# A fused encoder layer on one core: shorter routing, tokens gathered in tiles of 128 slots, three of the four tiles gathered inside the first experts' blocks

## What is computed

```python
def hierarchical_moe(hn, w_rg, w_re, w1, w3, w2):
    p_group = softmax(xf @ w_rg);  g_idx = argmax(p_group);  g_gate = p_group[g_idx]
    fine = (xf @ w_re).reshape(n, MOE_GROUPS, MOE_PER_GROUP)[g_idx]
    top_v, top_i = lax.top_k(fine, MOE_TOPK)
    gate = g_gate * jax.nn.softmax(top_v, axis=-1)
    ...
    def expert_block(args):
        xblk, e = args
        return (jax.nn.silu(xblk @ w1[e]) * (xblk @ w3[e])) @ w2[e]
    ...
    y = zeros((n + 1, d_)).at[slot_tok].add(yb * slot_w[:, None])[:n]
```

## Time and profile before

| | us |
|---|---|
| median of 3 runs | 2014.64 (2013.08 to 2017.55) |
| the profiled execution, device time | 2014.21 |
| its span, first to last instruction | 2012.3 |
| PE busy | 1893.8 (94%) |
| DVE busy | 831.5 (41%) |
| ACT busy | 510.1 (25%) |
| weights and all else moved by DMA | 556.63 MB, mean 277 GB/s |

### The profile page before, as it was taken

How to read it: one execution, slowest core, us unless ns; L and a number is a source line. 1 busy time by engine, 2 the same in 40 slices (tenths; PEclk the granted TensorE clock), 3 DMA queues, 4 the chain that set the end, 5 groups by cost and what they waited for, 6 DMA issues and landing times.

```text
span 2012.3 us, 24848 instructions
## 1 busy us (share of the span) xinstructions
PE 1893.8 (94%) x10000; PEld 1233.4 (61%) x10000; DVE 831.5 (41%) x1196; ACT 510.1 (25%) x727; POOL 50.4 (3%) x54
## 2 busy tenths in 40 slices
PE   6999999989899999999698999999999999999995
PEld 6888799889777779978643334434434433433342
DVE  4644454788644554335432232322322222232223
ACT  4444343644333444333210100000000000001001
POOL 0000000022210000000000000000000000000000
PEclk9999899989999999999798999999999999999997
DMA  7554445334565454425609999999999999999992
GB/s 269 166 169 155 131 162 185 120 115 144 123 145 160 161 188 153 162 81 190 265 3 425 428 428 428 429 428 429 428 429 429 428 428 429 429 428 428 429 429 107
DMA packets 106973, 556.63 MB, mean 277 GB/s; under 512 B 12336, under 2 KB 12568, under 8 KB 81176
## 3 DMA queue, kind: packets, MB, share of 16 engines
q1 hardware_dynamic: 96952, 423.51, 54.5%
q10 hardware_dynamic: 8928, 130.03, 15.2%
q0 software_dynamic: 1024, 2.10, 1.5%
HBM read 553.51 MB, written 2.10 MB: 276 GB/s over the span
## 4 chain that ended last, share of the span: by engine, by line
PE 82%; DMA 10%; DVE 5%; ACT 2%; issue 1%; POOL 0%; DVEq 0%; SPq 0%; ACTq 0%
PE ps L846 20%; DMA arena<-in_moe_w_dram 9%; PE ps L871 8%; PE ps L534 6%; PE ps L857 6%; PE ps L535 6%; PE ps L536 6%; PE ps L528 6%; PE ps L529 6%; PE ps L530 6%; PE ps L888 3%; PE ps L818 1%; PE ps L677 1%; PE ps L496 1%; DVE w_lo L1344 1%
## 5 line engine op out<-in xcount | busy, mean ns | idle before, releaser
L846 PE MATMUL ps<-arena 128*64 128x512 f32 x2048 | 505.7, 628 | 23.7 <-DMA arena<-in_moe_w_dram 23.2
L1344 DVE TENSOR_TENSOR w_lo<-arena,w_hi 128x1024 fp32r<-128x1024 f32 x264 | 319.3, 1253 | 291.4 <-ACT w_hi L989 290.9
L989 ACT ACTIVATE w_hi<-arena 128x1024 fp32r<-128x1024 f32 x264 | 264.4, 1052 | 331.6 <-PE ps L530 176.6
L846 PEld LDWEIGHTS ps<-arena 128*64 128x64 f32 x2048 | 137.3, 141 | 286.8 <-issue 266.6
L1895 DVE TENSOR_TENSOR arena<-ps,arena 128x1024 f32<-128x1024 f32 x128 | 156.5, 1225 | 222.4 <-PE ps L888 222.4
L871 PE MATMUL ps<-arena 128*64 128x512 f32 x1024 | 230.3, 603 | 0.6 <-DVE arena L1874 0.6
L871 PEld LDWEIGHTS ps<-arena 128*64 128x64 f32 x1024 | 75.7, 142 | 157.0 <-issue 156.3
L528 PE MATMUL ps<-x_hi,w_hi 128*128 128x256 f32 x512 | 147.1, 287 | 6.9 <-DVE w_lo L1344 6.9
L1889 DVE TENSOR_TENSOR d_lo<-ps,d_hi 128x512 fp32r<-128x512 f32 x64 | 41.2, 686 | 264.1 <-ACT d_hi L1242 264.1
L530 PE MATMUL ps<-x_hi,w_lo 128*128 128x256 f32 x512 | 146.3, 286 | 0.0
L529 PE MATMUL ps<-x_lo,w_hi 128*128 128x256 f32 x512 | 146.2, 286 | 0.0
(11 more groups left out here) (347 smaller groups left out, 2660.6 us busy)
## 6 DMA issues: line engine op xcount, KB each, us to landing
arena<-in_moe_w_dram SPq DMA_DIRECT2D x130, 2048.0 KB, 17.7
arena<-in_moe_w_dram ACTq DMA_DIRECT2D x62, 2048.0 KB, 14.2
arena<-in_w_in_dram SPq DMA_DIRECT2D x52, 1024.0 KB, 5.1
arena<-in_xa_wk_dram SPq DMA_DIRECT2D x16, 1024.0 KB, 5.1
arena<-in_xa_wv_dram SPq DMA_DIRECT2D x16, 1024.0 KB, 5.1
arena<-in_w_out_dram SPq DMA_DIRECT2D x16, 1024.0 KB, 5.1
arena<-in_xa_wq_dram SPq DMA_DIRECT2D x16, 1024.0 KB, 5.1
arena<-in_xa_wo_dram SPq DMA_DIRECT2D x16, 1024.0 KB, 5.1
```

Source lines behind the costliest of these rows:

```text
L846: last = mm(ps[rows_, m, :], xe[par][:, ECH * i + c, :], ring_up[m][i][:, c, :], start=(i == 0 and c < 2), stop=(i == ECH - 1 and c >= 2))
L989: fn(hi_ring[(2 * n + u) % 4][:], ring_a[i][:, 2 * u:2 * u + 2, :], ACT.Copy).then_inc(S["w_hi"], 1)
L1344: V.tensor_tensor(w_lo[i][:, 2 * u:2 * u + 2, :], ring_a[i][:, 2 * u:2 * u + 2, :], hi_ring[(2 * n + u) % 4][:].bitcast(F32), ALU.subtract ...
```

## The change

**Routing made shorter.** The logits of group n - 1 are made inside XO's group n (`logits`), and only those of the last group stand behind XO. The squares are summed by quarters on ACT between XO's splits (`part_square`). DVE's chain works on unscaled logits and on both token tiles and both experts at once (`hit01`, `slot01`, `fine4`). Its selection matrix `sel` is unscaled, and the norm goes into `hx`, a copy of `h` on ACT, scaled and with its columns regrouped, so that PE's weights are neighbouring columns.

**Gathering in tiles.** `gather(t, b, at)` makes one tile of 128 slots for one of four banks of features. Tile 0 is gathered ahead of expert 0, and DVE evicts its first 64 slots straight to `xe[0]` (`first_tokens`), while ACT evicts the tile to `xsT`. Tiles 1 and 2 are gathered by halves around the downs in blocks 1 and 2, tile 3 by one half ahead of the downs in each of blocks 3 and 4 (`gather_half`, evicted by `gathered`). Blocks 1 to 5 are written out for that, and the loops start later.

**Sums.** ACT's eviction of the up result (`up_out`) regroups its columns, reading PSUM at a stride of 4 elements, and `sums` reads neighbouring columns.

**Transfers.** The router's weights are loaded between the projections. The ups of expert 0 are issued between XO's last groups. The ups of experts 1 to 5 follow the downs of expert 0 directly, with no wait but that for their places, and the final gain is loaded after them. The program waits for the table (`tab_dve`) ahead of block 1 instead.

The diff, cut to its core:

```diff
@@ sync
-            for g in range(G_WO + 1, G_XO + 4):
+            for g in range(G_WO + 1, G_WQ + 1):
                 load_dense(g)
...
+            for g in range(G_WQ + 1, G_XO + 2):
+                load_dense(g)
+            sp.wait_ge(S["xs_o"], XA_H)
             for m in range(2):
+                load_dense(G_XO + 2 + m)
                 for i in range(0, ECH, 2):
                     load_up(0, 0, m, i)
             sp.wait_ge(S["chunk_used"], (G_XO + 4) * NCH)
             for i in range(0, ECH, 2):
                 load_down(0, i)
-            sp.wait_ge(S["row_pe"], 1)
-            sp.wait_ge(S["tab_dve"], 3)
+            for n in range(1, 6):
+                load_expert(n, n)
+            sp.wait_ge(S["g_pe"], 10)
             sp.dma_start(fgain, ...)
-            with sp.Fori(1, NE) as e:
+            with sp.Fori(6, NE) as e:
                 load_expert(e, e)
@@ tensor
             for n in range(4):
-                dense_split(G_XO + n, False, split[G_XO])
+                dense_split(G_XO + n, False, split[G_XO], part=[0])
                 if n >= 1:
                     group_turned(G_XO, n - 1, turn, 0)
+                dense_split(G_XO + n, False, split[G_XO], part=[1])
+                if n >= 1:
+                    logits(n - 1)
+                dense_split(G_XO + n, False, split[G_XO], part=[2, 3])
             group_turned(G_XO, 3, turn, 0)
...
+            logits(3)
...
-            for k_ in range(KT):
...
-                    last = mm(ps[:, 4 + k_ % 4, :], h[:, j, k_::KT], sel_r[:, j, :], start=(j == 0), stop=(j == NT - 1))
+            def gather(t, b, at):
+                for c in range(4):
+                    for j in range(NT):
+                        last = mm(ps[:, at, c * P:(c + 1) * P], hx[:, j, (4 * b + c) * P:(4 * b + c + 1) * P], sel[:, j, t * P:(t + 1) * P],
+                                  start=(j == 0), stop=(j == NT - 1))
+                return last
+            pe.wait_ge(S["hx_act"], NT)
+            pe.wait_ge(S["sel_dve"], 1)
+            for b in range(4):
+                gather(0, b, 4 + b).then_inc(S["g_pe"], 1)
+            def gather_half(t, half):
+                if t == 1 and half == 0:
+                    pe.wait_ge(S["sel_dve"], 2)
+                pe.wait_ge(S["g_dve"], 2 * t + half + 2)
+                for b in range(2):
+                    last = gather(t, 2 * half + b, 6 + b)
+                last.then_inc(S["g_pe"], 1)
...
-                        last = mm(bank(2 + m, ECH, EB)[:, c, :], up_ev[:, m, c::ECH], stack[:], start=True, stop=True)
+                        last = mm(bank(2 + m, ECH, EB)[:, c, :], up_ev[:, m, c * P:(c + 1) * P], stack[:], start=True, stop=True)
...
             block_n(0, None, 0)
             slot_rows()
-            block_n(1, 0, 1)
-            with pe.Fori(0, NE // 2 - 1) as e:
+            pe.wait_ge(S["tab_dve"], 2)
+            block_n(1, 0, 1, ((1, 0), (1, 1)))
+            block_n(2, 1, 0, ((2, 0), (2, 1)))
+            block_n(3, 2, 1, ((3, 0),))
+            block_n(4, 3, 0, ((3, 1),))
+            block_n(5, 4, 1)
+            with pe.Fori(0, NE // 2 - 3) as e:
@@ scalar
+            def part_square(n, j):
+                fn(arena(88, 512), h[:, j, GW * n:GW * (n + 1)], ACT.Square, accum_out=...).then_inc(S["sq_part"], 1)
...
+            for j in range(NT):
+                fn(hx[:, j, :].rearrange("p (k q) -> p k q", k=KT), h[:, j, :].rearrange("p (q k) -> p k q", k=KT), ACT.Copy,
+                   scale=st[:, 40 + j:41 + j]).then_inc(S["hx_act"], 1)
...
-                fn(up_ev[:, m, :], ps[:, m, :], ACT.Copy)
+                fn(up_ev[:, m, :].rearrange("p (c q) -> p c q", c=ECH), ps[:, m, :].rearrange("p (q c) -> p c q", c=ECH), ACT.Copy)
@@ vector
+            def select(a, z):
+                for j in range(NT):
+                    last = V.tensor_scalar(sel[:, j, a:z], iota[:, a:z], slot01[:, j, 0:1], None, ALU.is_equal)
+                step(last)
+                for j in range(NT):
+                    last = V.scalar_tensor_tensor(sel[:, j, a:z], iota[:, a:z], slot01[:, j, 1:2], sel[:, j, a:z], ALU.is_equal, ALU.add)
+                last.then_inc(S["sel_dve"], 1)
+            def first_tokens(b):
+                dve.wait_ge(S["g_pe"], b + 1)
+                V.tensor_tensor(xe[0][:, 4 * b:4 * b + 4, :], bank(4 + b, 4, P)[:, :, 0:EB], bc_last(ffn_gain[:, 4 * b:4 * b + 4], EB),
+                                ALU.mult).then_inc(S["g_dve"], 1)
+            def gathered(t, half):
+                dve.wait_ge(S["g_pe"], 2 * t + half + 3)
+                for b in range(2):
+                    ...
+                    last = V.tensor_tensor(xsT[:, k:k + 4, t * P:(t + 1) * P], bank(6 + b, 4, P), bc_last(ffn_gain[:, k:k + 4], P), ALU.mult)
+                last.then_inc(S["g_dve"], 1)
+            select(0, P)
...
+            first_tokens(0)
+            select(P, SLOTS)
+            first_tokens(1)
```

More of the change, by code:

```diff
@@ L810, in _ @@
             mm(o_[:, 1, :], ones, hit[:, 0, :], start=False, stop=True)
-            mm(o_[:, 2, :], ones, hits, start=True, stop=True).then_inc(S["r_pe"], 1)
-            pe.wait_ge(S["tab_dve"], 1)
-            for k_ in range(KT):
-                if k_ >= 4:
-                    pe.wait_ge(S["g_act" if k_ % 2 == 0 else "g_dve"], (k_ - 4) // 2 + 1)
-                for j in range(NT):
-                    last = mm(ps[:, 4 + k_ % 4, :], h[:, j, k_::KT], sel_r[:, j, :], start=(j == 0), stop=(j == NT - 1))
-                last.then_inc(S["g_pe"], 1)
@@ new lines, in _, with slot_rows @@
+            for b in range(4):
[7 more added lines that the diff above has]
+                last.then_inc(S["g_pe"], 1)
+            def slot_rows():
+                pe.wait_ge(S["g_act"], 4)
+                for k in range(2):
+                    for j in range(NT):
+                        mm(ps[:, 5, (2 * k + j) * P:(2 * k + j + 1) * P], slot01[:, j, k:k + 1].to_broadcast([P, P]), ident[:], start=True, stop=True)
+                pe.wait_ge(S["selg_dve"], 1)
+                for j in range(NT):
+                    last = mm(ps[:, 4, :], onesm, sel_g[:, j, :], start=(j == 0), stop=(j == NT - 1))
@@ L900, in block_n @@
                         down(back, i)
+                for half in halves[1:]:
+                    gather_half(*half)
                 up(n, 0, 2, par)
@@ L1711, in _ @@
             xa_out_lo(3)
[L1712 to L1716 removed]
+            for n in range(5):
+                if n < 4:
+                    low(G_XO + n, (0, 1))
+                if n >= 1:
+                    dense_add(G_XO + n - 1, n - 1)
+                    turned(0, xT, 2, part=range(2 * n - 2, 2 * n))
+                if n < 4:
+                    low(G_XO + n, (2, 3))
+            V.memset(onesm, 1.0)
+            V.memset(lgrp, LOWEST)
+            dve.wait_ge(S["sq_part"], 8)
+            step(V.tensor_reduce(st[:, 0:NT], st[:, 44:52].rearrange("p (j g) -> p j g", g=4), AX.X, ALU.add))
+            rsqrt(NT, 1.0 / D)
+            V.tensor_copy(st[:, 40:42], st[:, 24:26]).then_inc(S["rms_dve"], 1)
             dve.wait_ge(S["r_pe"], 1)
             dve.wait_ge(S["route_in"], 16)
[L1719 to L1723 removed]
+            raw = bank(6, NT, 36)
+            V.tensor_copy(logit, raw)
+            step(V.tensor_copy(lgrp[:, :, 0:NG], raw[:, :, 0:NG]))
             for j in range(NT):
@@ L1895, in add, with block_n @@
                 V.tensor_tensor(hv, flat(ps[:, b0:b0 + 2, :]), hv, ALU.add).then_inc(S["c_add"], 1)
-            def block_n(back, s_back, par, then):
+            def block_n(back, s_back, par, then, halves=()):
                 gating(back, s_back)
-                if then:
+                for half in halves[:1]:
+                    gathered(*half)
+                if then and (1, 1) not in halves:
                     tokens(back + 2, start_of(back + 2), par)
@@ L1902, in block_n @@
                 down_lo(back)
+                for half in halves[1:]:
+                    gathered(*half)
+                if (1, 1) in halves:
+                    dve.wait_ge(S["g_dve"], 6)
+                    tokens(back + 2, start_of(back + 2), par)
                 for q in range(4):
```

290 lines of the change are left out of this document (145 added, 145 removed).

## The result

The changed kernel takes **1977.35 us** (median of four runs, 1975.5 to 1978.75) against 2014.49 for the kernel before, measured beside it (2013.08 to 2017.55). The ratio is 0.9815, with a 95% interval of 0.9803 to 0.9827: 37.1 us less. The prediction was 1979.4, in a range of 1968 to 1993. The profiled execution took 1976.2 us with a span of 1974.4.

The account below looks back on a forecast made before the run. The prediction held the experts bound by the gapless 428 GB/s weight stream: start - 47.0, gaps + 15.0 (stream's end - 32.0), tail - 2.8, so - 34.8 on the profiled 2014.2 gave 1979.4 us; range 1968 to 1993.

Parts of the forecast that it names:

- 1. XO and the logits: Output projection: 48 logits move into XO (+ 5.4 us), 16 stay; DVE's chain starts at 986.3 instead of 990.11, - 3.8.
- 2. The chain: DVE's routing up to gathering: finding hits 6.1 to 3.6 us, the rest 7.7 to 3.9; gathering at 996.4, - 9.6 in all.
- 3. Gathering: Tile 0 ahead of expert 0: 8.9 us (7.2 to 14.4) instead of 29.61; first up at 1005.3 instead of 1038.37.
- 4. The start: Expert 1's first transfer, freed of SP's waits, starts the weight stream at 1008.8 instead of 1055.85: - 47.0 us.
- The rival that something would hold the transfers back in SP's queue: Expert 1's first piece leaves only at block 1, at 1024.4, 15.6 later; time 1990 us, chance 0.04.
- 5. The gaps: Blocks 1 to 3, at 36.1, 33.1 and 29.5 us, starve the weight stream: + 15.0 us, bounds 8 and 25.
- 6. The steady blocks: Later expert blocks gain nothing from shorter sums, because the weight stream sets 29.4 us.
- 7. The tail: Behind the last weights: shorter sums of experts 30 and 31, less possible low clock; - 2.8 us, range 0 to 6.
- Stream broken longer: Lower clock in all of tile 0 (+ 5.5) and the half tiles of blocks 1 and 2 (+ 14.4): 1998 us, chance 0.12.
- Tighter: Weight stream gaps of 8 us instead of 15 and a tail gain of 6: 1969 us, chance 0.10.
- `hx` late: ACT's strided copies ahead of gathering cost four times, 7.5 us each, making all behind 4.8 later: 1984 us, chance 0.04.
- Slower: Short sums drop PE's clock, so PE bounds all blocks, up to 34.6 us each: from 2014 us on, chance 0.03.

Follow-up runs that it names:

- the run without half tiles: Changed kernel with each half tile of slots 128 to 511 cut to two plain products of 128 columns, so tiles 1 to 3 aren't gathered: 1965.65 us.
- the two runs on the half tiles: Changed kernel with each half tile's 32 products replaced by two plain ones, of 512 columns (1970.13 us) or of 128 columns (1965.65 us).
- the stream alone: Kernel before with only expert 1's up transfers issued ahead of SP's two waits for slot rows and table: 2001.34 us.

## Why the prediction was right

**What bounds it.** Right: the stream sets the steady experts before and after (428 GB/s from 1160 on), and the sums alone gave only 3.0 us.

**1. XO and the logits.** The chain was to start 3.8 earlier, at 986.3. It starts at 984.38 (5.7 earlier). The forecast let it start with the norm, at 986.2, and the norm was ready at 984.5. XO's last turning was put at 980.8 (975.44 + 5.4) and came at 979.75, within its scatter. The step gave the reason as 48 logits moving into XO at 5.4 us and 16 left behind. The run with all of them behind XO starts its chain at 985.0, so moving them was not the reason: the price of 12.45 us in the earlier trace rows fell to 8.90 without it.

**2. The chain.** Gathering was put at 996.4 and started at 994.65, all of it owed to step 1: from the chain's start to it, 10.1 us were forecast and 10.3 measured. One sum of the step doesn't come out: eleven operations of 0.2 us, less 0.3, take 1.9 from 6.1 and leave 4.2, not 3.6. The trace has 3.6 (984.38 to 987.99), so the number was met and its working wasn't.

**3. Gathering.** Forecast 8.9 us, measured 10.21 in this trace. Of the eleven kernels with this gathering, six took 8.76 to 8.88, four 10.21 to 10.34, and the one with `hx` twice 9.39 for the 60 instructions that its trace has. Here the low clock lasted from 994.6 to 1000, not the 3.4 us taken over from the earlier trace rows. The forecast lies at the lower of two values. The first up came at 1004.86 (forecast 1005.3).

`hx` was taken at 1.88 us a copy with a cover of 2.7 times that. It took 3.69, twice the price, and stayed hidden. The 1.88 was of another function that writes to PSUM; the squares in the changed kernel, which read neighbouring elements and write to SBUF, take 0.63 us for 512 columns, which makes 2.5 for 2048 as an estimate. The Trainium skill, "SBUF — State Buffer", section "Door 1: The DMA port swizzle (why `[64,N]` ≈ `[32,N]`)", which says that each access to a new line of 16 bytes pays, agrees with the trace here (3.69 us), and with the sums' weight loads (216 ns instead of 328 in the earlier trace rows).

Of PSUM the Trainium skill says in the same passage only that access which is not contiguous slows matmuls; the prediction set it against ACT's strided read of PSUM in `up_out` too. There the trace shows no price: 598 ns for an eviction of 128x512, where it was 598 ns before. The groups of instructions by line have both:

```profile
L1291 ACT ACTIVATE arena<-ps 128x512 f32<-128x512 f32 x64 | 38.2, 598 | 358.9 <-PE ps L878 358.9
L889 PEld LDWEIGHTS ps<-stack,arena 128*128 128x128 f32 x512 | 68.6, 216 | 32.6 <-issue 32.6
```

**4. The start.** Forecast 1008.8, measured 1008.48. The rival that something would hold the transfers back in SP's queue didn't come. The first up (1004.86 for 1005.3) and the way from it to the first transfer (3.6 us for 3.5) both fit.

**5. The gaps.** Forecast 15.0, measured 15.0, but not made up as told. Block 1 was to take 36.1 us and took 33.85: the 3.0 us of low clock after the wait for the table weren't there. PE stood 1.7 us and went on at 1.00 (1.94 and 1.93 in the chain). The pauses were to be at block 1's second up (4.6 us) and at the downs (2.1). In single microseconds the low ones are 1029 to 1032 and 1034 to 1039, and only one of them is empty:

```profile
1029.00:1030.00 1.00, 1.00 (x10) 0.98 (x9) 0.00 (x0) 0.00 (x0) 0.00 (x0) 1.00 0.43 180
1030.00:1031.00 1.00, 1.00 (x11) 1.00 (x10) 0.00 (x0) 0.00 (x0) 0.00 (x0) 1.00 1.30 262
...
1036.00:1037.00 1.00, 1.00 (x8) 0.29 (x4) 0.00 (x0) 0.00 (x0) 0.00 (x0) 1.00 0.04 16
```

Block 1 and what is ahead of it lost less than the 7.7 forecast, some 6 us, block 2 lost 5.1 (forecast 4.1) and block 3 2.5 (3.2), from windows between their first ups. The remaining 1.3 lies behind 1120. Two errors met here, the low clock that didn't come and a loss that isn't idleness, and that 15.0 met 15.0 is luck. Taking the steady share of 1.01 as full, the transfers were idle for some 7 us in the four windows above, and by bytes 14.1 us are missing in them. The rest are stretches in which they are busy and move less, like 1030 to 1040 in the run without half tiles, at a share of 0.99 with 362 GB/s. That the gaps grow and shrink with PE's excess over 29.4 us a block is shown by the two runs on the half tiles (11.2 us less of PE, 10.0 less of gaps) and by the old sums (12.4 more, 12.3 more). The excess of blocks 1 to 4 of the changed kernel is 9.7 us in all, though, and where the other 5 of the 15.0 come from is shown only for the 1.4 us lost ahead of block 1. The pauses of 4.6, 2.1 and 1.0 were only argued, and their places are not what the trace shows.

**6. The steady blocks.** Right, no gain: 428 GB/s with PE waiting 49.0 us for weights in all where it waited 23.2.

**7. The tail.** This was the mis-sized term: 2.8 us forecast, 5.5 measured. The step counted the sums and took the downs at 9.92 us as given. In fact the sums gave 2.0 (4.5 to 2.5 us from their start to the downs) and the downs 2.8. The last 0.7 lies within the scatter: the last sums start from 1.8 to 5.1 us behind the stream's end in kernels with the same code. Over nine other traces with the new sums and the new order the tail is 37.5 to 40.4, so a gain of about 4 is what repeats.

**The rivals.** *Stream broken longer* didn't come: of its low clock only the first 5.4 us of the gathering were there, and the half tiles ran at full clock (3.77 us). The old sums in the changed kernel gave nearly as many gaps, 27.3, in another way. *Tighter* (gaps of 8) came only where the half tiles were cut. *`hx` late* needed four times the price and had two. *Slower*, a PE that the short sums slow down, is refuted by its opposite: the last downs behind the new sums are faster (7.11 us), and the steady blocks stayed with the stream.

Sum: - 47.4 + 14.9 - 5.5 = - 38.0 on the span (- 37.9 before rounding), against - 34.8.

## What to carry to other kernels

An edit that shortens work which another resource hides is worth little alone, and more once a second edit has put a part of that work on the path: here 3.0 and 16.8 us. When a stream starts earlier, count how far the blocks ahead exceed its time per block, since most of that excess comes back as gaps; a later start didn't save them here, where the consumer waits for the first piece. Where the quarters of a contraction become ready one after another, try them as the outermost loop, with a wait for each: 64 logits that took 12.45 us took 8.90 that way.

## What the runs showed of the hardware

**The clock behind strided weights.** The last downs stand behind the last sums. In the three traces with sums on weights at a stride of 4 (before, the stream alone, the old sums in the change) they took 9.92, 8.60 and 9.79 us, and the granted clock was 0.50 in their first 3 us. In all eleven with sums on neighbouring columns they took 7.11, at 1.00. The windows of the changed kernel with the old sums show it (last sums, then the downs' first stretch):

```profile
1955.20:1959.00 3.80, 3.80 (x16) 3.69 (x16) 1.65 (x2) 0.38 (x1) 0.00 (x0) 0.90 0.00 0
1959.70:1963.00 3.30, 3.30 (x8) 0.95 (x10) 0.64 (x2) 0.00 (x0) 0.00 (x0) 0.50 0.00 0
```

PE counts as busy in them, but its 16 products of 64 columns are spread over 3.9 us instead of 1.9. It isn't so behind all such sums: in a steady block of the kernel before the steps behind them took 1.87 and 6.87, and with the old sums in the change one of the four up steps named above kept its 1.87. So strided weights cost their own time and at times that of what follows; what decides between the two was not tried. The prediction had only the first.

**Short and long waits.** After 1.7 us of waiting PE went on at 1.00, after 9.5 us the next three steps ran at 0.50 and took nearly twice their time. The wait alone doesn't tell it: behind one of 1.02 us the logits of the kernel before were at 0.56, behind 1.06 us those of the changed kernel at 0.88. **A strided copy** by ACT from SBUF (elements 64 bytes apart) took 3.69 us for 128x2048 where squares of neighbouring elements, written to PSUM, took 1.88, and a read of PSUM at a stride of 16 bytes took no more than a plain one (598 ns). **Transfers** can be busy at 0.99 and move 362 GB/s where they sustain 428; what sets that rate when few pieces are on their way was not tried.
